# A three-block transformer kernel: weight loads, splits and gate projections moved across stage boundaries

## The reference, cut to what matters

```python
def gated_mixer(h, w_in, b_gate, ...):
    proj = h @ w_in
    ...
    gates = jax.nn.sigmoid(proj[..., o0:] + b_gate).reshape(B, S, 2, D)
    out_a = diff_attention(qa, ka, va, lam, lam_init, subln_w)
    out_b = chunk_band_attention(qb, kb, vb, rel_bias)
    merged = gates[:, :, 0] * (out_a @ w_branch_a) + gates[:, :, 1] * (out_b @ w_branch_b)
    return merged @ w_out

def second_block(x, w_in, ...):
    h = x @ w_in[l]
    ...
    o_hg = o_hg * lax.rsqrt(jnp.mean(jnp.square(o_hg), axis=-1, keepdims=True) + RMS_EPS)
    ...
    mixed = jnp.concatenate([o_nsa * jax.nn.silu(nsa_z),
                             o_sb * jax.nn.silu(sb_z),
                             o_hg.astype(x.dtype) * jax.nn.silu(hg_z)], axis=-1)
    x = layer_norm_2(ALPHA * x + (mixed @ w_out[l]).astype(x.dtype), ln_g[l], ln_b[l])
```

## Time and profile before

| | |
|---|---|
| median of 3 runs | 2325.35 us (2321.66 to 2329.87) |
| the profiled execution's own time | 2329.57 us |
| its span | 2327.3 us |
| PE busy / weight loads / DVE / ACT / POOL | 2053.2 / 1655.3 / 1688.0 / 1256.4 / 343.1 us |
| TensorE clock, mean of the profiled run | 0.93 |

### The profile page before, as it was taken

The page is one execution under the profiler, slowest core; times in us unless marked ns, Lnnn a source line. Parts: engine busy times, 40 slices in busy tenths (PEclk is TensorE's granted clock), DMA queues, the critical chain, the costliest instruction groups (busy, mean ns, idle before and its releaser), DMA issues. The chain is left out here.

```text
span 2327.3 us, 29904 instructions
## 1 busy us (share of the span) xinstructions
PE 2053.2 (88%) x10236; PEld 1655.3 (71%) x10236; DVE 1688.0 (73%) x1967; ACT 1256.4 (54%) x1397; POOL 343.1 (15%) x190
## 2 busy tenths in 40 slices
PE   3988969983999999999999999999973799888868
PEld 2766748862788888888888888888852666667756
DVE  4463642166799999999999999999966176344856
ACT  3343442312677777777777777777742244243431
POOL 0202123301011211211112112111110000000320
PEclk9998989995999999999999999999986897699978
DMA  5214032415899999999999999999954400101121
GB/s 190 55 36 145 19 96 77 140 64 192 305 361 395 378 384 386 376 390 383 373 393 374 380 393 373 386 384 381 386 171 131 103 1 1 55 28 55 47 64 73
DMA packets 201618, 519.00 MB, mean 223 GB/s; under 512 B 21974, under 2 KB 81502, under 8 KB 201196
## 3 DMA queue, kind: packets, MB, share of 16 engines
q1 hardware_dynamic: 191212, 482.68, 55.9%
q0 software_dynamic: 9504, 34.61, 5.7%
q10 hardware_dynamic: 832, 0.80, 0.1%
HBM read 494.41 MB, written 29.41 MB: 225 GB/s over the span
## 5 line engine op out<-in xcount | busy, mean ns | idle before, releaser
L1607 DVE TENSOR_TENSOR piece_lower<-piece,moe_upper 128x2048 fp32r<-128x2048 f32 x384 | 870.4, 2287 | 29.0 <-ACT moe_upper L1527 29.0
L1527 ACT CAST moe_upper<-piece 128x2048 fp32r<-128x2048 f32 x384 | 734.0, 1914 | 281.1 <-PE bank L1459 269.1
L1457 PE MATMUL bank<-moe_upper,x_hi 128*128 128x512 f32 x1536 | 620.4, 404 | 2.5 <-DVE x_hi L1601 2.5
L1459 PE MATMUL bank<-moe_upper,x_hi 128*128 128x512 f32 x1536 | 606.0, 395 | 0.0
L1458 PE MATMUL bank<-piece_lower,x_hi 128*128 128x512 f32 x1536 | 601.7, 392 | 0.0
L1457 PEld LDWEIGHTS bank<-moe_upper,x_hi 128*128 128x128 f32 x1536 | 290.1, 189 | 68.0 <-DVE piece_lower L1607 2.9
L1458 PEld LDWEIGHTS bank<-piece_lower,x_hi 128*128 128x128 f32 x1536 | 290.1, 189 | 63.1
L1459 PEld LDWEIGHTS bank<-moe_upper,x_hi 128*128 128x128 f32 x1536 | 289.8, 189 | 62.7
L1412 POOL DMA_INDIRECT mixed<-moe_y,moe_dst x32 | 104.7, 3273 | 27.5 <-issue 27.5
L135 PE MATMUL bank<-x_hi,ahead_lower 128*128 128x512 f32 x248 | 100.6, 406 | 0.0
L1410 POOL COPY moe_dst<-row 128x1 uint32 (+1 forms) x32 | 6.6, 208 | 609.5 <-ACT moe_y L1516 609.5
(11 more groups left out here) (551 smaller groups left out, 3491.1 us busy)
## 6 DMA issues: line engine op xcount, KB each, us to landing
piece<-in_w_exp_in_dram SPq DMA_DIRECT2D x256, 1024.0 KB, 7.6
piece<-in_w_exp_out_dram SPq DMA_DIRECT2D x128, 1024.0 KB, 9.5
ahead<-in_w_in_dram SPq DMA_DIRECT2D x18, 512.0 KB, 4.7
ahead<-in_w_in_dram SPq DMA_DIRECT2D x3, 2048.0 KB, 8.3
ahead<-in_w_in_dram SPq DMA_DIRECT2D x4, 1536.0 KB, 6.9
merge_raw<-in_w_in_dram SPq DMA_DIRECT2D x8, 512.0 KB, 5.7
ahead<-in_w_out_dram SPq DMA_DIRECT2D x2, 2048.0 KB, 9.3
out_w<-in_w_out_dram SPq DMA_DIRECT2D x2, 2048.0 KB, 8.1
```

The lines of the kernel that those rows point to most:

```text
L1457: nc.tensor.matmul(to, hi[:, f, :], upper[u][:, t, cols], start=f == 0 and not biased, stop=False)
L1459: done = nc.tensor.matmul(to, lo[:, f, :], upper[u][:, t, cols], start=False, stop=f == NK - 1)
L1527: nc.scalar.copy(upper[h % SPLIT][:, :, :], ring[s][:, :, :]).then_inc(hi_ready, 1)
L1607: nc.vector.tensor_tensor(lower[s][:, :, :], ring[s][:, :, :], upper[h % SPLIT][:, :, :].bitcast(F32), ALU.subtract).then_inc(lo_ready, 1)
```

## The change

- **diff to band.** `heads_stage` takes `following`, loads that SP issues when the last unit is projected. Diff loads band's value weights with it. `transpose_heads_stage` with `values` (diffnorm) casts and splits these weights and projects the first two of four value tiles ahead of the head transposes; band (`projected_values`) projects the other two only. The value buffers become shared ones (`k.v`, `k.v_upper`).
- **band to merge.** Band's `following` loads the first merge tiles. Merge's first iteration is taken out of the loop, its weights are cast and split in three parts, the lower halves on DVE. The bias casts go from ACT to DVE.
- **nsakv to nsa.** Unit 0's query weights are loaded, split and projected (24 matmuls) in nsakv, into bank 3, ahead of the products that follow the tanh chain. Nsa starts with unit 1's weights.
- **nsa to sb.** Nsa loads the query and key weights of sb; nsat casts and splits them ahead of its copies.
- **hgates.** The first 384-wide weight tile is cast and split in three parts.
- **hg, hgt, silu.** The lower halves of z go from POOL to DVE. Tiles 0 to 3 are projected in hg, 4 and 5 in `hgrn_norm_stage` (new) ahead of the transposes, 6 and 7 in silu. Sigmoids and products of tiles 0 to 3 are in `hgrn_norm_stage` too, on ACT and DVE; silu's POOL block is gone. The load of w_out's first half waits for tile 5.
- The 3 MB write of a bias table to memory (`spread_row` of z_t5) goes from diffnorm to out1, behind the load of w_out's second half.

```diff
                     dma.then_inc(w_in[u % 2], 16)
+            if following is not None:
+                sp.wait_ge(projected, projected0 + units * projections)
+                following(sp)
 
...
-                project(0, n, c)
+            elif projected_values:
+                for i in v_rows:
+                    for c in range(NK):
+                        last = split_product(nc, k.bank[3 + i][:, :], k.x_parts[:, c, i * P:(i + 1) * P],
+                                             v_w[:, c, :], c == 0, c == NK - 1)
+                    last.then_inc(v_ps, 1)
...
+                for m in range(4):
+                    part = slice(P * m, P * m + P)
+                    dve.wait_ge(next_hi, m + 1)
+                    split_lower(nc.vector, k.ahead[:, :, part], next_upper[:, :, part], k.ahead_lower[:, :, part])
+
...
             if heads:
+                nc.vector.tensor_tensor(sq[:, :, :], o, o, ALU.mult)
+                if values is not None:
+                    lower_part(0)
+                    lower_part(1)
...
+            if values is not None:
+                for h in range(4):
+                    pe.wait_ge(v_lo, h + 1)
+                    for i in range(2):
+                        for c in (2 * h, 2 * h + 1):
+                            last = split_product(nc, k.bank[4 + i][:, :], k.x_parts[:, c, i * P:(i + 1) * P],
+                                                 v_w[:, c, :], c == 0, c == NK - 1)
+                        if h == 3:
...
+            def iteration(p, f):
+                pe.wait_ge(w_lo, f * 2 - 1)
+                pe.wait_ge(gates, f * 2 + 1)
+                for g in range(2):
+                    gate_products(p, g)
+                pe.wait_ge(w_lo, f * 2)
+                pe.wait_ge(merged, f + 1)
+                branch_products(p)
...
+            for g in range(2):
+                pe.wait_ge(first_lo, g + 1)
+                gate_products(0, g)
+            pe.wait_ge(first_lo, 3)
+            branch_products(0)
+            iteration(1, 1)
+            with pe.Fori(1, NK // 2) as q:
                 for p in range(2):
-                    f = q * 2 + p
...
-            upper_parts(0, 0, (k.ahead_in, ahead_loads))
+            act.wait_ge(k.ahead_in, ahead_loads)
+            for part in FIRST:
+                nc.scalar.copy(upper[0][:, part, :], raw[0][:, part, :]).then_inc(w_hi, 1)
             act.drain().then_inc(gates, 1)
             upper_parts(1, 1, (w_in[1], 64))
...
+            for n, part in enumerate(FIRST):
+                dve.wait_ge(w_hi, n + 1)
+                split_lower(nc.vector, raw[0][:, part, :], upper[0][:, part, :], w[0].lo[:, part, :]).then_inc(first_lo, 1)
...
+            dve.wait_ge(bias_in, 48)
+            nc.vector.tensor_copy(k.bias[:, :], full[:, :])
+            for rows, groups in ((slice(NE, 3 * NE), (1, 2)), (slice(2 * NE, 3 * NE), (2,))):
+                dve.drain()
+                for g in groups:
+                    bias_remainder(g)
+                dve.drain()
+                for g in groups:
+                    nc.vector.tensor_copy(k.bias[NE * g:NE * g + NE, :], full[NE * g:NE * g + NE, :])
+            dve.drain()
...
+            pe.wait_ge(lo_ready, l0 + 6)
+            for f in range(NK):
+                split_product(nc, k.bank[FIRST_BANK][:, :], q_w[:, f, :], k.x_parts[:, f, :], f == 0, f == NK - 1)
...
+Z_EARLY, Z_BETWEEN = 6, 4
...
-                project(1 + t // 2, t % 2)
+                if t < N - 1:
+                    project(1 + t // 2, t % 2)
...
             arguments(0)
+            lower_part(0)
...
+                    lower_part(1 + t // 2)
                 if t > FAR:
                     take_both(t, LEVELS[t - 1]).then_inc(lev_done, 1)
             dve.drain()
...
+def hgrn_norm_stage(nc, k, A, z, o, m_t):
...
+            for f in range(Z_EARLY, NK):
+                sp.dma_start(z.raw_rest[:, f - Z_EARLY, :].rearrange("p (c n) -> p c n", n=P),
+                             column_tiles(w2, Z_FIRST[f])).then_inc(z.loaded[4], 16)
+            sp.wait_ge(z_ps, Z_EARLY)
+            load_ahead(sp, k, column_tiles(A["w_out_2"][0], 0, 512))
+
+        @block.tensor
+        def _(pe):
+            for f in range(Z_BETWEEN, Z_EARLY):
+                for c in range(NK):
+                    last = split_product(nc, k.bank[6 + f % 2][:, :], z.w[f][:, c, :], k.x_parts[:, c, :],
+                                         c == 0, c == NK - 1)
+                last.then_inc(z_ps, 1)
+            pe.wait_ge(ready, n + 1)
+            for c in range(TILES):
+                for i in range(NT):
+                    last = nc.tensor.transpose(k.bank[c][:, i * P:(i + 1) * P], o[:, i, c * P:(c + 1) * P], k.ident)
+                last.then_inc(transposed, 1)
+
+        @block.scalar
+        def _(act):
+            act.wait_ge(sum_ready, n + 1)
+            nc.scalar.activation(std[:, :], sums[:, :], ACT.Sqrt).then_inc(std_ready, 1)
+            for f in range(Z_BETWEEN):
+                nc.scalar.activation(sg[:, f, :], z.early[:, f, :], ACT.Sigmoid).then_inc(sg_ready, 1)
+            for f in range(Z_BETWEEN, Z_EARLY):
+                act.wait_ge(z_ps, f + 1)
+                nc.scalar.copy(z.early[:, f, :], k.bank[6 + f % 2][:, :])
+            act.wait_ge(weight_in, 16 * n + 16)
+            for c in range(TILES):
+                act.wait_ge(transposed, t0 + c + 1)
+                nc.scalar.activation(m_t[:, NK - TILES + c, :], k.bank[c][:, :], ACT.Copy, scale=wcol[:, c:c + 1])
+
```

More of the change, by code:

```diff
@@ L584, in heads_stage @@
             k.units.done[x] for x in ("w0_in", "w_split", "projected", "evacuated", "v_hi", "zeroed"))
-        in0 = (in0, k.units.done["w1_in"])
+        in0 = (in0 - done * loads, k.units.done["w1_in"])
+        split0, projected0 = split0 - done * projections, projected0 - done * projections
         BANKS = (2, 7)
@@ L588, in heads_stage @@
         STEPS = items.per_unit - 1
+        ahead_loads = k.ahead_loads
+        v_next, vp0 = v0 + NT, k.units.done["v_ps"]
         block = st.block()
@@ L592, in _ @@
         def _(sp):
-            for u in range(units):
+            for u in range(done, units):
                 if u == 1 and values is not None:
-                    sp.wait_ge(v_ps, v0 + NT)
+                    sp.wait_ge(v_ps, vp0 + len(v_rows))
                 if u >= 2:
@@ L626, in next_unit @@
                 pe.wait_ge(evacuated, evacuated0 + u * 2 + 2)
[L628 removed]
+            if early:
                 for h in range(4):
@@ L798, in _ @@
         def _(act):
+            if next_upper is not None:
+                act.wait_ge(k.ahead_in, ahead_loads)
+                for m in range(4):
+                    part = slice(P * m, P * m + P)
+                    nc.scalar.copy(next_upper[:, :, part], k.ahead[:, :, part]).then_inc(next_hi, 1)
+            if values is not None:
+                act.wait_ge(k.ahead_in, ahead_loads)
+                for h in range(4):
+                    part = slice(2 * h, 2 * h + 2)
+                    nc.scalar.copy(k.v_upper[:, part, :], k.ahead[:, part, :]).then_inc(v_hi, 1)
             if heads:
```

361 lines of the change are left out of this document (214 added, 147 removed).

## The result

The changed kernel takes 2285.54 us (median of four executions, 2281.83 to 2289.32) against 2325.93 us for the kernel before (four, 2321.66 to 2329.87): a ratio of 0.9824, 95% interval 0.9811 to 0.9838, 40.4 us less. A second measurement beside nine executions of before gave 2283.72 us and 0.9814 (0.9796 to 0.9833), 43.6 us less. The forecast was 2276.8 us (a difference of 48.6), in a range of 2261 to 2295.

The account below looks back on a forecast made before the run. The prediction priced PE's idle time and restarts at six boundaries. Its terms sum to -48.6 us: 2329.57 profiled becomes 2281.0, less 4.2 for the median, 2276.8; range 2268 to 2287, with most of rivals 1 and 2 2261 to 2295.

Parts of the forecast that it names:

- the key stage's boundary: Keys to sparse attention: first scores come earlier, with unit 0's query weights loaded, split and projected beforehand; -7.7 us.
- Merge: Band to merge: first product 5.8 us earlier and no wait left before the second iteration; -15.5 us.
- the cover: Merge: DVE's bias chain releases PE at 341.4, PE asks at 346.6, so 5 us to spare.
- Diff to band: Diffnorm and band: norm ends 5.7 us later, but 48 matmuls, 10.9 us, leave band; -7.4 us taken.
- (a): HGRN stage: POOL's subtractions no longer draw out three DVE operations; some -3.4 us, 2.4 of it let through.
- (d): HGRN's last products: 12 half-clock matmuls ahead of them go, -5.1 us, but these products run at half clock; -3.9.
- (c): HGRN stage: tile 4's half projection between the last products goes, -2.7 us, of which the chain gives 2.3.
- (b): HGRN stage: two more subtractions on DVE, in the chain argument, product, query; +2.3 us.
- rival 2: The covers fail in merge, diffnorm, HGRN, silu and sparse attention's start: some 17 us back, 2294 us; chance 0.20.
- b without a: HGRN: DVE's added subtractions cost time while the gain from removing POOL's contention fails to come; 3.4 + 2.3 us.
- rival 1: Third sparse unit: clock stays up, 17.8 us more gained, half if for half the unit; 2264 us, chance 0.13.
- signs of being wrong: Bias chain releasing a merging sum; third sparse unit far from 54 us; first sparse units above 45; out1 awaiting its load.

Follow-up runs that it names:

- early-split kernel: Changed kernel with DVE's subtractions of HGRN gate tiles 1 to 3 issued sooner: 2276.98 us, ratio 0.9794.
- HGRN filling: Kernel with early HGRN splits and 24 unread products in the third sparse unit, plus 18 unread wide products ahead of HGRN's last products: 2261.11 us, ratio 0.9718.
- both splits: Two variants of the changed kernel: HGRN gate-tile subtractions issued earlier on DVE (2276.98 us), or those of tiles 0 to 3 back on POOL (2282.18 us).
- HGRN as before: Changed kernel with the HGRN attention, its norm stage and silu as before the change: 2286.77 us, ratio 0.9831.
- merge's load late: Changed kernel with merge's first weights loaded in the transposing stage just ahead, as before; thirds and DVE's casts stay: 2285.4 us, ratio 0.9827.
- values in band: Changed kernel with all four of band's value products in the band stage, weights still loaded and split in front: 2293.25 us, ratio 0.985.
- bias casts: Changed kernel with the expert biases' casts in merge back on ACT, ahead of the second iteration's sigmoids: 2300.82 us, ratio 0.9888.
- queries late: Changed kernel with the first sparse unit's query weights loaded, split and projected in sparse attention, as before: 2285.89 us, ratio 0.9824.
- copies first: Changed kernel with ACT's scaled copies of the first sparse unit's queries ahead of the cast of the next unit's weights: 2285.08 us, ratio 0.9823.

## Why the prediction came out as it did

**Right, term by term.** Stick-breaking (-4.6, measured -4.7), gates (-3.9; PE's wait before its first product went from 7.20 to 3.36 us), the norm stage that got longer (+3.8, +3.9), silu (-7.0, -7.3), the key stage's boundary (-7.7; -8.9 between the profiles, -7.3 by undoing it alone). All were sums of idle time before a first product, with casts and splits in thirds, and durations from the rows of before. Of these only the key stage's term was undone by itself; the others rest on two profiles. That the table's row of the gates agrees to 0.1 us is partly luck: the stick-breaking stage in it varies by 1.9 us between kernels that leave it alone (83.8 to 85.7).

**Merge: right in sum.** The -15.5 were -16.8, 1.5 of it band attention itself (86.5 to 85.0 us from its first scores to the transposes behind it; the granted clock fell there once before, 0.93 from 285 to 309 us, and not after). The bias chain was forecast to end at 339, 23.6 us behind the stage's start (315.4); it ended at 331.6, 26.2 behind its start (305.4). Casts were cheaper (1.22 for at most 1.9), but DVE's operations beside POOL's subtractions were drawn out: the two casts at 319.11 took 6.78 us where one takes 1.22, and a subtraction 4.32 for 2.28. The Trainium skill ("GPSIMD Engine Reference", Key points) says that GpSimd contends with VectorE's instructions in a 2-port perf mode and with those that have two SBUF inputs. That these casts run in such a mode is not shown by any row; that a cast with one input is drawn out is shown (the two took 4.3 us more than alone, beside POOL's 8.37). DVE's last step (333.99 + 0.16) released PE at 334.2. The first iteration took 19.0 us, not 18.0, and PE came to the branch products that need the release at 337.6, so 3.5 of the cover's 5 us were left.

**Diff to band: -7.4 forecast, -5.6 measured.** Up to band's first value product the working holds within 0.9 us (the value products in the norm stage start 3.5 us in, as worked out, and take 13.6 us for 13.1). The step that was too large is "10.9 us, are gone from it": band's products before its first scores fell by 9.8 us, 35.7 to 25.9, since the restart at half clock behind the barrier cost more this time (band's first 24 products took 8.0 us for 7.0). These 0.9 and 1.1 us are the miss.

**HGRN: the step that failed.** Of terms (a) to (d), -6.3 in sum, nothing came: the stage kept its 65 us. Up to the last 48 products, where (a) to (c) stand for -2.4, it got 2.7 us longer (51.3 to 54.1); behind that, (d) gave -2.6 for -3.9. (a) and (b) were priced as additions to the level chain: POOL's contention off, 2.4 of 3.4; two DVE subtractions on, 2.3. The working asked how long a subtraction is and what it delays on DVE. It did not ask what waits for it on PE: the tile's half projection stands in order in front of the level's shared products, and DVE issues the subtraction only behind the next level's arguments, which (at the second and third wait) come late themselves, behind PE's products of the level before. So each split was late by its place, 1.44 + 2.33 + 1.96 = 5.7 us of idling, and the clock fell twice. The prediction listed among rival 2's prices "b without a"; it had no row for a wait of PE on a DVE split. The early-split kernel shows the size: 7.6 us up to the last products, 6.7 us in the median. With it the stage takes 57.4 us, -8.0 where -6.3 was forecast. In (d) a smaller size was off: the second 24 products were put at "some 4" us at half clock and took 5.3.

**The sparse units: two rivals cancelled.** Rival 2's cold start is there, +2.2 us in the first unit for its 3; a fall of the clock at the end of the second unit adds 2.8, which no rival had; rival 1's shorter stretch of half clock in the third unit is there too, -5.3. The sum, -0.3, looks like "nothing happened", and agrees with the forecast's 0 by luck. Two of the prediction's signs of being wrong came so without the time leaving its range: the third unit far from 54 us (48.8), and a first unit above 45 (53.3). The second says little, since the first unit took 51.1 us already before.

So: forecast -48.6; -40.4 and -43.6 measured. HGRN's 6.4 and diff to band's 1.7 account for 8.1, merge and the keys gave 2.5 back and the gates' stage 1.9; the stretch between merge and the keys took 1.7, and the start of the kernel moves by some 3 us on its own.

## What the runs showed of the hardware

The clock does not only fall behind idling. In the third sparse unit it was 0.50 with PE busy for 52.98 of 55.12 us, and it was 1.00 when 24 products of 512 columns were put between the narrow ones: 9.6 us less for more work. It had fallen at the end of the second unit, with no idling of PE over 0.72 us in the 8 us before. The stretch in after, from there to the clock's return:

```profile
1917.60:1961.50 43.90, 42.64 (x145) 31.78 (x145) 23.98 (x84) 15.34 (x58) 0.00 (x0) 0.50 0.01 2
```

The Trainium skill ("TensorE: Matmul & The Clock Gate", Why this matters for your kernels) warns of idle gaps between bursts of matmuls. The HGRN filling is of that kind (idling of 2.83 us filled, the 48 products behind it 5.0 us shorter), though it adds wide products as well and can't tell the two apart. The third unit is outside of it: the longest idling of PE that its rows show is 0.59 us in after and 0.55 in the kernels with 55.1 us. That added products of this width bring the clock back is shown; why narrow ones lose it is not.

The same instructions of the third unit took 48.8 us in five kernels (after, both splits, HGRN as before, merge's load late) and 55.1 in two (values in band, bias casts), which are alike in the whole stage; it was 54.2 before, 48.1 with the queries late and 54.1 with the copies first. What upstream decides it was not found: it may be the moment at which the stage starts, and this was not tried. In both kinds the clock falls at the same place, 90.2 to 90.5 us behind the stage's first scores; where the unit takes 48.8 us it is back 44 us later, where it takes 55.1 it stays at 0.50 to the end of the unit. It means that 6 us can appear in a stage that neither of two kernels touches, and come back in part in others: of the 9.5 and 17.1 us of the two experiments some 2 are left of it.

Filling the start of sparse attention made the first unit 3 us shorter and the other two longer. Whether a start at full clock is paid back later by rule or by chance is open.

## What to carry to other kernels

Where a small operation is moved to another engine, its length is the smaller question: look up which in-order engine waits for its result and what has been queued in front of it at its new place. A row of idling on the consumer, released by it, is the sign, and moving it into a stretch where its new engine idles can be worth more than its duration (here 7.6 us for three operations of 1.2). Where the granted clock is at its lower level beside narrow products, wide products that nothing reads are worth trying; the same at the start of sparse attention gained nothing. Compare stages, not only medians, before a difference is ascribed to an edit. The best version here that is told apart from its base, with early splits and the fillings in the third sparse unit and ahead of HGRN's last products, takes 2261.11 us, 2.8% less than before and 1.0% less than the changed kernel.
